# Second block's up-projection: one 512-column matmul in place of two 256-column ones, halves added on the way out of PSUM

## The reference

```python
m = rmsnorm_2(h, norm_mlp_pre[i])
m = jnp.square(jax.nn.relu(jnp.einsum('bsd,df->bsf', m, w_up[i])))   # 1024 -> 4096
m = jnp.einsum('bsf,fd->bsd', m, w_down[i])                          # 4096 -> 1024
h = h + rmsnorm_2(m, norm_mlp_post[i])
```

## Time and profile before

| | |
|---|---|
| runs | 1909.38, 1911.18, 1911.8 us; median 1911.18 us |
| profiled execution | time 1909.38 us, span 1909.4 us |
| TensorE (PE) | 98% of the span busy, 16004 matmul records |
| DVE | 70% busy |
| ACT | 52% busy |
| the chain that ended last | PE 84%, DVE 10%, ACT 4% |

### The profile page before, as it was taken

One profiled execution on the slowest core, in us unless ns is written; L12 is line 12 of the kernel. 1 busy time (PEld: TensorE's weight loads), 2 busy tenths in 40 slices (PEclk: granted clock), 3 DMA queues, 4 the chain that ended last, 5 costly groups with the idle time before them and its releaser, 6 DMA issues.

```text
span 1909.4 us, 36805 instructions
## 1 busy us (share of the span) xinstructions
PE 1871.4 (98%) x16004; PEld 1854.5 (97%) x16004; DVE 1343.1 (70%) x1652; ACT 998.8 (52%) x1243; POOL 133.0 (7%) x110
## 2 busy tenths in 40 slices
PE   8999999999999999999999999999999999899999
PEld 8999999999999999999999999998999999899998
DVE  7755787785558655787776556888865589777655
ACT  6443545564437544545565445767534367654443
POOL 1000000000000000000000000264000006600000
PEclk9999999999999999999999999999999999899999
DMA  8655554465555555535545555423566544237651
GB/s 266 207 189 189 165 171 149 159 210 189 188 192 173 204 199 199 186 119 187 179 155 199 199 199 169 155 89 113 180 200 199 183 139 135 72 114 240 199 193 51
DMA packets 246532, 329.56 MB, mean 173 GB/s; under 512 B 6246, under 2 KB 218788, under 8 KB 246372
## 3 DMA queue, kind: packets, MB, share of 16 engines
q1 hardware_dynamic: 246018, 326.79, 51.9%
q0 software_dynamic: 96, 0.26, 0.1%
q10 hardware_dynamic: 258, 0.16, 0.0%
HBM read 326.14 MB, written 1.05 MB: 171 GB/s over the span
## 4 chain that ended last, share of the span: by engine, by line
PE 84%; DVE 10%; ACT 4%; issue 1%; DMA 1%; ACTq 0%; DVEq 0%; SPq 0%
PE work L2061 19%; PE work L2063 19%; PE work L2062 19%; PE acc L2061 9%; PE acc L2063 8%; PE acc L2062 8%; DVE w_lo L1334 3%; ACT w_hi L795 2%; DVE ra L1347 1%; DVE fa L1784 1%; PE work L2208 1%; DMA raw<-in_w_in_dram 1%; PE acc L2130 1%; DVE fa L1860 0%; DVE fa L1386 0%
## 5 line engine op out<-in xcount | busy, mean ns | idle before, releaser
L1334 DVE TENSOR_TENSOR w_lo<-raw,w_hi 128x2048 fp32r<-128x2048 f32 (+2 forms) x313 | 697.4, 2229 | 109.9 <-ACT w_hi L795 108.0
L2061 PE MATMUL work<-x_rows,w_hi 128*128 128x256 f32 x2560 | 712.3, 278 | 8.0 <-DVE w_lo L1334 4.9
L2062 PE MATMUL work<-x_rows,w_hi 128*128 128x256 f32 x2560 | 707.9, 277 | 0.0
L2063 PE MATMUL work<-x_rows,w_lo 128*128 128x256 f32 x2560 | 707.7, 276 | 0.0
L795 ACT ACTIVATE w_hi<-raw 128x2048 fp32r<-128x2048 f32 (+2 forms) x313 | 578.4, 1854 | 150.6 <-PE work L2063 67.2
L2061 PEld LDWEIGHTS work<-x_rows,w_hi 128*128 128x128 f32 x2560 | 483.8, 189 | 11.3 <-issue 6.2
L2062 PEld LDWEIGHTS work<-x_rows,w_hi 128*128 128x128 f32 x2560 | 483.8, 189 | 0.3
L2063 PEld LDWEIGHTS work<-x_rows,w_lo 128*128 128x128 f32 x2560 | 483.8, 189 | 0.0
L2061 PE MATMUL acc<-ra,w_hi 128*128 128x256 f32 x1352 | 372.4, 275 | 0.0
L2063 PE MATMUL acc<-ra,w_lo 128*128 128x256 f32 x1352 | 372.0, 275 | 0.0
L2062 PE MATMUL acc<-ra,w_hi 128*128 128x256 f32 x1352 | 372.0, 275 | 0.0
(11 more groups left out here) (318 smaller groups left out, 2267.9 us busy)
## 6 DMA issues: line engine op xcount, KB each, us to landing
raw<-in_ffn_w_gu_dram SPq DMA_DIRECT2D x88, 1024.0 KB, 5.1
raw<-in_w_in_dram SPq DMA_DIRECT2D x52, 1024.0 KB, 5.4
raw<-in_ffn_w_down_dram SPq DMA_DIRECT2D x44, 1024.0 KB, 5.0
raw<-in_w_up_dram SPq DMA_DIRECT2D x32, 1024.0 KB, 5.4
raw<-in_w_down_dram SPq DMA_DIRECT2D x32, 1024.0 KB, 4.9
raw<-in_w_mla_out_dram SPq DMA_DIRECT2D x8, 1024.0 KB, 5.5
raw<-in_w_o_dram SPq DMA_DIRECT2D x8, 1024.0 KB, 5.0
raw<-in_w_ple_gate_dram SPq DMA_DIRECT2D x8, 1024.0 KB, 5.0
```

Of the source, the lines that this page charges most:

```text
L1334: v.tensor_tensor(w_lo[:, s, 0:n], raw[:, r, 0:n], w_hi[:, s, 0:n].bitcast(F32), ALU.subtract).then_inc(lo_done.sem, 1)
L2061: pe.matmul(dst, ah, bh, start=start and i == 0, stop=False, skip_group_check=not group)
L2062: pe.matmul(dst, ah, bl, start=False, stop=False, skip_group_check=not group)
L2063: last = pe.matmul(dst, al, bh, start=False, stop=stop and i == len(pairs) - 1, skip_group_check=not group)
```

## The change

In steps 4 to 15 of both layers the three products of a tile become two matmuls. The rows of `xh` and `xl` are laid side by side, so that the 512 columns of `x_both[:, k, :]` are one contiguous read; the high weights are loaded once and the 512 columns go through them into a whole PSUM bank (columns 0 to 255: high by high; 256 to 511: high by low). The low weights then take the 256 high columns into columns 0 to 255 of the same bank. So a step fills two banks, one for each `m`, and has two units. ACT copies the 256 columns of the second half of both banks to `us` (`low_halves`), DVE adds them to the first half, gives the two banks back, and multiplies by the row of inverse norms in a third instruction. Steps 0 to 3 are as before.

```diff
-X_SIZE, X_ROW, X_AT = 4124, 256, (28, 2076)
+UP_WIDE = 4
+X_SIZE, X_AT = 4124, 28
...
-    names += [("up", j) for j in range(MLP_STEPS)]
+    for j in range(MLP_STEPS):
+        names += [("up", j)] if j < UP_WIDE else [("up", j, m) for m in range(2)]
...
-        xh, xl = (rows_at(x_rows, at, KD, X_ROW) for at in X_AT)
+        x_both = cut(x_rows, X_AT, KD, 2 * T)
+        xh, xl = x_both[:, :, 0:T], x_both[:, :, T:2 * T]
...
+        low_half = Signal(semaphore("low_half"), 0, MLP_STEPS - UP_WIDE)
...
-                        return unit_ready, U2["up", j]
+                        return unit_ready, U2[("up", j) if j < UP_WIDE else ("up", j, 1)]
...
+                def low_halves(j):
+                    units = [U2["up", j, m] for m in range(2)]
+                    for m, u in enumerate(units):
+                        act.wait_ge(unit_ready.sem, unit_ready.after(here, u))
+                        last = act.activation(us[:, j % 2, m, :], bank2(u)[:, 1, :], ACT.Copy)
+                    last.then_inc(low_half.sem, 1)
                 for j in range(MLP_STEPS):
+                    if j >= UP_WIDE:
+                        low_halves(j)
...
+                    units = [U2["up", j, m] for m in range(2)]
+                    v.wait_ge(*low_half.at(here, j - UP_WIDE))
+                    for m, u in enumerate(units):
+                        v.tensor_tensor(gs[:, p, m, :], us[:, p, m, :], bank2(u)[:, 0, :], ALU.add).then_inc(unit_taken.of(u), 1)
+                    for u in units:
+                        taken(here, u)
+                    chain(here, v.tensor_tensor(gs[:, p, :, :], gs[:, p, :, :], over(scale_row, 2), ALU.mult))
                 for j in range(MLP_STEPS):
-                    scaled(here, u, gs[:, p, :, :])
-                    taken(here, u)
+                    up_in(j)
...
+            def wide(here, c, units):
+                w = weights(here, c)
+                for m, u in enumerate(units):
+                    free(here, u)
+                    for k in range(KD):
+                        pe.matmul(bank(u), w[0][:, k * 256 + m * P:k * 256 + m * P + P], x_both[:, k, :], start=k == 0, stop=False,
+                                  skip_group_check=True)
+                        last = pe.matmul(bank(u)[:, 0:T], w[1][:, k * 256 + m * P:k * 256 + m * P + P], xh[:, k, :],
+                                         start=False, stop=k == KD - 1, skip_group_check=True)
+                    last.then_inc(unit_ready.sem, 1)
...
-                    if j < MLP_STEPS:
+                    if j < UP_WIDE:
                         project(here, up_chunk(j), U2["up", j])
+                    elif j < MLP_STEPS:
+                        wide(here, up_chunk(j), [U2["up", j, m] for m in range(2)])
```

More of the change, by code:

```diff
@@ L1977, in _, with up_in @@
                 make_rstd(here, "mlppre")
+                def up_in(j):
+                    p = j % 2
+                    if j < UP_WIDE:
+                        scaled(here, U2["up", j], gs[:, p, :, :])
+                        taken(here, U2["up", j])
+                        return
+                    units = [U2["up", j, m] for m in range(2)]
[5 more added lines that the diff above has]
+                    chain(here, v.tensor_tensor(gs[:, p, :, :], gs[:, p, :, :], over(scale_row, 2), ALU.mult))
                 for j in range(MLP_STEPS):
-                    u = U2["up", j]
                     p = j % 2
-                    scaled(here, u, gs[:, p, :, :])
-                    taken(here, u)
+                    up_in(j)
                     v.scalar_tensor_tensor(hid[:, p, :, :], gs[:, p, :, :], 0.0, gs[:, p, :, :], ALU.max, ALU.mult).then_inc(
```

## The result

The changed kernel takes 1916.58 us (median of 8 runs, 1913.89 to 1917.23), the kernel before 1910.71 us beside it (8 runs, 1908.18 to 1912.26). The ratio is 1.0028, with a 95% interval of 1.0019 to 1.0037: **slower by 5.9 us** between the medians, about 5.3 by the ratio, and between 3.6 and 7.1 by its interval. The prediction of 1908.6 us was wrong, and its range, which ended at 1913.0, doesn't hold the result.

What follows compares the result with a forecast made beforehand. PE's matmul pace in the feed-forward steps was taken as the bound. Its 2.6 us gain, with nothing elsewhere, came off the 1911.2 us median: 1908.6 us, called no change, range 1905.0 to 1913.0.

Steps and rivals of the forecast that it cites:

- the term for PE: Up pieces: a wide and a narrow matmul take 333.5 ns, 6.7 less than three of 256; 2.6 us over 384 pairs.
- Rival C: Wide matmuls at L2124 run below one column per clock, up to 5.6 us slower: 1916.8 us; chance 0.06.
- A: Up-piece matmuls lose their extra altogether, the pair taking 320.0 ns: 7.8 us less, 1903.4 us; chance 0.10.
- B: The up matmuls' extra goes with columns, 6.7 ns per 256, so nothing changes: 1911.2 us; chance 0.13.
- E: Long up moves overlap, a column costing less than a clock; the pair takes 266.8 ns: 1883.0 us; chance 0.01.
- D: Fewer free PSUM banks make PE wait in up pieces and its clock fall: 1922.1 us; chance 0.02.
- the bound: Steady feed-forward steps: PE busy for all 148 us at 2.4 GHz, so the distance between matmul starts sets the end.
- ACT's copies: Two 256-column copies from PSUM per step, before the weight splits, 0.8 us together, waiting for no one.
- DVE's additions: Two 256-column additions with one PSUM operand per step, 0.9 us together, following ACT's copies without new idle time.
- SyncE's load: The load released by DVE's first weight split starts 0.9 us later, with 5 us left before ACT needs its chunk.
- the second split: The second weight split of a step, on ACT, waits for an up piece on PE and doesn't move.
- the shorter ring: A step takes two of four PSUM banks; they are back 8.4 us before PE needs them, so no wait.

Runs made afterwards that it cites:

- run 5: Changed kernel with the wide move cut to lengths from 256 to 512 columns by step, first layer wide first, second in turns: 1896.48 us, one execution.
- run 2: Changed kernel with each step's 16 wide matmuls first, then its 16 narrow ones: 1911.24 us, ratio 1.0008 to the kernel before.
- run 3: Changed kernel with each 512-column matmul issued as two of 256 into the halves of the same bank: 1909.46 us, ratio 1.0002 to the kernel before.
- run 1: Changed kernel with UP_WIDE = 16, so the new row layout but no 512-column moves: 1908.81 us, ratio 0.9999 to the kernel before.
- runs 6 and 9: Changed kernel with three 256-column matmuls; 6 begins moved rows or weights earlier, by layer: 1916.77 us; 9 shifts both: 1914.12 us; one execution each.
- run 8: Changed kernel with each matmul loading 64 (first layer) or 32 (second) columns of weights instead of 128: 1914.70 us, one execution.

## Why the prediction was wrong, point by point

**The step that failed** is the term for PE: "I take one column per clock on top of the row that is nearest in kind (same arena moved, same weights): 113.4 + 256 x 0.417 = 220.1 ns. With a narrow matmul at 113.4 the pair is 333.5 ns". The slope was about right (run 5), both bases were wrong: the wide matmul takes 233.7 ns and the narrow one 118.8. The 113.4 ns of the earlier trace rows isn't the price of the operands but the settled pace of 256-column moves at these places, and the change breaks that fit twice, in the wide move by its length and in the narrow one by what stands around it. Why these lengths and places fit is not known. In the result's sum that is 13.6 + 5.4 - 6.7 = 12.3 ns a pair, a loss in place of a gain of 6.7 ns.

The rows to tell it by were there. The earlier trace rows show 13.5 ns extra at two lengths. I took that for the general case of *other* operands and the 113.4 for the case of these. Read the other way, with 13.5 ns for both, the pair is 226.8 + 120.2 = 347.0 ns and the change 2.6 us slower: the right sign, and not quite half of the size. And the run at 1357.82 (shown under run 2) has the operands of the earlier trace rows themselves at 119 ns for ten steps.

**Rival C** had the time, 1916.8, but by chance, and not the mechanism. It put the loss on L2124 alone, with a wide matmul of 236.7 ns or more that takes more than one clock per column; 233.7 was enough, because the narrow matmul didn't stay at 113.4, and run 5's columns cost about one clock. **A**, **B** and **E** fell with the 233.7 ns. TensorE: Matmul & The Clock Gate of the Trainium skill, section Back-to-back issue gap, gives N/2.4 + 2.5 ns for an isolated matmul, 215.8 at 512 columns, and about 131 in a stream. The traces show 224 to 241 between starts in a stream, so neither figure is met here. **D** fell too: PE waits nowhere in the stage and holds clock 1.00; the failure that the same page of the Trainium skill describes under A second HAM failure mode: psum-queue depth-cycling doesn't show in these traces.

**Right**, and shown by run 3 as a whole: the bound; ACT's copies (0.64 us, 0.8 predicted) and DVE's additions (0.75, 0.9 predicted) lie beside PE's work; SyncE's load comes 0.85 us later (0.9 predicted) behind the same cover; the second split waits for PE as before; no wait of the shorter ring on PE. Right by run 1: the layout costs nothing.

**A slip beside the sum.** The prediction put the profiled execution at 1909.38 us, "its span", and called it the fastest of the three; the table ahead of it has the same. But the time of the kernel before is 1.75 to 1.93 us above its span in every run from which both were taken together, so a span of 1909.4 belongs to an execution of about 1911.2 us, the median, and the two equal numbers were a coincidence. The forecast didn't hang on it, since the difference was carried to the median.

## What to carry to other kernels

A pace that is better than that of other rows of the same kind may be a fit that a change can lose, as here, so price a new form from the ordinary rows, and price its unchanged neighbours from them too. Where PE is the bound, read distances between starts, also in the pieces behind the changed one, and see how many matmuls a run needs to settle: the narrow ones of the change, each alone between two wide ones, never did. Fewer and longer matmuls are no gain by themselves: here the smaller count was bought with a larger extra on each of those left.

## What the runs showed that I had not expected

- The step between 256-column fp32r matmuls with a weight load each is 113.3 ns at some places of rows and weights in their arenas and 113.9 to 120 at others, to the same 0.001 us of a piece each time (runs 6 and 9). Four columns' shift of the moved rows costs 0.30 us on a piece of 5.44, 5.5%; in all 24 steps that would be 7.2 us, more than the change lost.
- A matmul's extra isn't its own: 256-column matmuls behind a 512-column one need some ten matmuls to come back to 113 ns (run 2), as the kernel before needed ten at the start of a run (1358.13 to 1359.32), and the untouched down piece paid 0.026 us a step for its neighbour.
- Halving the weights, or quartering them, doesn't make a 512-column move cheaper in general (227 to 236 ns, run 8).
